# Which buffers the next weights take, when they are split, and how an opening is shared: a chain of residual blocks on one core

## The reference

```python
mod = (silu(c) @ w_mod + b_mod).reshape(-1, 9, 1024)          # and modc, the same from c_ctx
ada_in(x, mod, j, g)  = rmsnorm(x, g) * (1 + mod[3j+1]) + mod[3j]
ada_out(x, z, mod, j, g, r) = x + r * mod[3j+2] * rmsnorm(z, g)
x  = ada_out(x,  swiglu(ada_in(x,  mod,  0, ...), ffn_w_in, ffn_w_out), mod,  0, ..., 0.5)
xc = ada_out(xc, swiglu(ada_in(xc, modc, 0, ...), ffn_w_in, ffn_w_out), modc, 0, ..., 0.5)
...   # an mLSTM and pooling mixer over both, its output product w_out, a second swiglu
```

```python
x = x + 0.5 * rms_norm(swiglu_ffn(rms_norm(x, g0), w_gate, w_up, w_down), p0)
m = hybrid_mixer(rms_norm(x, g1), ...)     # ends in:
#   branch_d = einsum('bsgw,gwd->bsgd', branches, w_branch)     three branches
#   merged   = sum(sigmoid(gates) * branch_d, axis=2)
#   m        = merged @ w_out
x = x + rms_norm(m, p1)
x = x + 0.5 * rms_norm(swiglu_ffn(rms_norm(x, g2), ...), p2)
```

## Time and profile before

| | |
|---|---|
| median of three runs | 2121.56 us |
| the profiled execution | 2123.9 us |
| its span, first to last instruction | 2122.1 us |
| mean granted TensorE clock | 0.990 |
| TensorE busy | 2050.0 us (97%) |
| VectorE busy | 1320.1 us (62%) |
| ScalarE busy | 1034.8 us (49%) |
| DMA | 392.90 MB, 185 GB/s on average |

### The profile page before, as it was taken

How to read it: one execution, slowest core, us unless ns; L and a number is a source line. 1 busy time by engine, 2 the same in 40 slices (tenths; PEclk the granted TensorE clock), 3 DMA queues, 4 the chain that set the end, 5 groups by cost and what they waited for, 6 DMA issues and landing times. The chain is left out here.

```text
span 2122.1 us, 27560 instructions
## 1 busy us (share of the span) xinstructions
PE 2050.0 (97%) x11092; PEld 1720.9 (81%) x11092; DVE 1320.1 (62%) x2135; ACT 1034.8 (49%) x1444; POOL 25.9 (1%) x51
## 2 busy tenths in 40 slices
PE   7999999998989999999999989999999999998998
PEld 5899899987767787888897868888888898777886
DVE  3555656655774657555687786555655677877553
ACT  4445465435454544444535644444544535655442
POOL 1000000000000000000000000000000000000000
PEclk9999999999999999999999999999999999999999
DMA  9885576654256756655543465554756443365551
GB/s 353 274 286 180 198 237 209 203 196 161 80 179 209 242 174 194 203 170 187 193 150 105 138 208 178 181 179 149 239 179 217 165 140 124 120 218 165 190 183 49
DMA packets 281758, 392.90 MB, mean 185 GB/s; under 512 B 9580, under 2 KB 175900, under 8 KB 281504
## 3 DMA queue, kind: packets, MB, share of 16 engines
q1 hardware_dynamic: 277472, 379.62, 53.5%
q0 software_dynamic: 3184, 9.04, 1.4%
q10 hardware_dynamic: 976, 2.49, 0.3%
HBM read 390.06 MB, written 1.05 MB: 184 GB/s over the span
## 5 line engine op out<-in xcount | busy, mean ns | idle before, releaser
L1932 DVE TENSOR_TENSOR wlo<-raw,whi 128x1024 fp32r<-128x1024 f32 x650 | 781.3, 1222 | 491.1 <-ACT whi L1360 489.2
L1360 ACT ACTIVATE whi<-raw 128x1024 fp32r<-128x1024 f32 x650 | 673.0, 1056 | 605.7 <-PE bank L802 359.5
L800 PE MATMUL bank<-whi,xTh 128*128 128x512 f32 (+1 forms) x1344 | 535.2, 398 | 20.0 <-issue 6.8
L802 PE MATMUL bank<-whi,xTl 128*128 128x512 f32 (+1 forms) x1344 | 524.8, 390 | 0.0
L801 PE MATMUL bank<-wlo,xTh 128*128 128x512 f32 (+1 forms) x1344 | 524.8, 390 | 0.0
L800 PEld LDWEIGHTS bank<-whi,xTh 128*128 128x128 f32 x1344 | 255.8, 190 | 79.0 <-issue 15.5
L802 PEld LDWEIGHTS bank<-whi,xTl 128*128 128x128 f32 x1344 | 255.2, 190 | 53.8
L801 PEld LDWEIGHTS bank<-wlo,xTh 128*128 128x128 f32 x1344 | 255.8, 190 | 49.5
L764 PE MATMUL bank<-xTh,whi 128*128 128x256 f32 x696 | 198.1, 285 | 0.8 <-DVE wlo L1932 0.7
L764 PE MATMUL bank<-xTl,whi 128*128 128x256 f32 x696 | 196.9, 283 | 0.0
L764 PE MATMUL bank<-xTh,wlo 128*128 128x256 f32 x696 | 196.9, 283 | 0.0
(11 more groups left out here) (358 smaller groups left out, 2339.3 us busy)
## 6 DMA issues: line engine op xcount, KB each, us to landing
raw<-in_w_in SPq DMA_DIRECT2D x68, 1024.0 KB, 5.2
raw<-in_ffn_w_in SPq DMA_DIRECT2D x132, 512.0 KB, 6.7
raw<-in_ffn_w_gate SPq DMA_DIRECT2D x88, 512.0 KB, 4.2
raw<-in_ffn_w_up SPq DMA_DIRECT2D x88, 512.0 KB, 5.4
raw<-in_ffn_w_down SPq DMA_DIRECT2D x40, 1024.0 KB, 4.9
raw<-in_w_mod SPq DMA_DIRECT2D x36, 1024.0 KB, 6.9
raw<-in_ffn_w_out SPq DMA_DIRECT2D x30, 1024.0 KB, 5.1
raw<-in_w_out SPq DMA_DIRECT2D x12, 1024.0 KB, 4.9
```

Source lines behind the costliest of these rows:

```text
L800: e.matmul(o, hi[:, kc, sl], wh[:, c], start=at == 0 and k == 0, stop=False)
L802: ins = e.matmul(o, lo[:, kc, sl], wh[:, c], start=False, stop=fin)
L1360: e.activation(m.wh[t.slot[q]][:, 0:width], m.raw[:, u % NRAW, j * width:(j + 1) * width], ACT.Copy).then_inc(m.whi_done, 1)
L1932: e.tensor_tensor(m.wl[t.slot[q]][:, 0:width], m.raw[:, u % NRAW, j * width:(j + 1) * width], m.wh[t.slot[q]][:, 0:width].bitcast(F32), AL ...
```

## The change

Four edits. (1) `widen` gets an argument `due` apart from `at`, and slots 18 to 22 are added with the key q0 - 0.5 and the same due time, q0 + 2. (2) Both engines set `limit` to piece 5 before `last` of the output product, and `merge` lifts it when it ends. (3) In the opening, VectorE scales and shifts token tile 3 (and ScalarE only copies it), VectorE adds the first bias between its two normalizations, `mod` settles the one before it between its two halves, and TensorE settles behind each tile's transposes. (4) The modulation pieces ahead of groups 2 and 3 go ahead of groups 8 and 9; `x` is loaded behind group 3 and normalized beside groups 6 and 7; POOL loads the gains at k = 7.

```diff
-    def widen(self, slots, kind, key, at=None, once=False):
+    def widen(self, slots, kind, key, at=None, once=False, due=None):
         at = len(self.subs) if at is None else at
+        due = at if due is None else due
...
-                self.guard[s] = (b, n + 1, at, at - 0.5)
+                self.guard[s] = (b, n + 1, due, at - 0.5)
...   # Tables.walk (and TensorE's and VectorE's loops alike)
         for g in range(2, NG):
-            if 2 + g < EARLY:
-                self.mod(MODS[2 + g])
+            if 4 <= g < EARLY:
+                self.mod(MODS[g])
...   # Tables.mixer
-        self.widen((18, 19, 20, 21, 22), "bank", ("mg", l, 1, 1), q0 + 2, True)
+        self.widen((18, 19, 20, 21, 22), "bank", ("mg", l, 1, 1), q0, True, q0 + 2)
...   # Pool
-            if k == 6:
+            if k == 7:
...   # Tensor.mod
             ins.then_inc(full if kh else m.mod_half, 1)
-        self.settle()
+            if kh == 0:
+                self.settle()
...   # Tensor.first_block
                 self.turned(("sh0", 2 + i), half, m.zc[:, i, :])
-            self.settle()
+                self.settle()
...   # Scalar.first_block
-            for i in range(2):
-                self.shift(("sh0", 2 + i), half, 0, 1, m.cTh, i)
-        e.dma_start(m.x[:, :, :], ...).then_inc(m.ld_x, 16)
+            self.shift(("sh0", 2), half, 0, 1, m.cTh, 0)
+            full = m.fullb[:, self.n.half % 2, :].rearrange("p (c n) -> p c n", c=4)
+            self.evacuated("sh0", 3, half)
+            self.hi(m.cTh[:, 4 * half:4 * half + 4, 128:256], full)
+            self.n.half += 1
...
-            if g < 4:
-                self.normalize(m.x[:, g - 2, :], m.z[:, g - 2, :], loaded=m.ld_x)
+            if g == 3:
+                e.dma_start(m.x[:, :, :], ...).then_inc(m.ld_x, 16)
+            if g in (6, 7):
+                self.normalize(m.x[:, g - 6, :], m.z[:, g - 6, :], loaded=m.ld_x)
...   # Scalar.mixer and Vector.mixer
             # at the end of merge(half)
+            self.limit = len(self.t.subs)
...
+        self.limit = self.t.first["wo2", l, 0] + 5
         self.last(4, ...)
...   # Vector.first_block
-        for i in range(2):
-            self.normalize()
+        self.normalize()
+        self.mod()
+        self.normalize()
         for half in range(2):
+            if half:
+                self.mod()
             self.mod()
-            self.mod()
-            if half:
-                self.force(4)
-            self.settle()
-            self.force(2)
+            self.force(2 + 2 * half)
+            self.settle()
+            self.evacuated("mod2", half, 0)
+            self.evacuated("mod2", 2 + half, 0)
+            bank, free = self.filled("sh0", 3, half)
+            full = m.fullb[:, (self.n.half + 1) % 2, :].rearrange("p (c n) -> p c n", c=4)
+            if half:
+                e.wait_ge(m.xt_done, 2)
+            for c in range(4):
+                k = 4 * half + c
+                ins = e.tensor_scalar(full[:, c, :], bank[:, c * 128:c * 128 + 128], m.gcol[:, 0, 1, k:k + 1],
+                                      m.modc[:, 0, 0, 1, k:k + 1], ALU.mult, ALU.add)
+            ins.then_inc(free, 1)
```

More of the change, by code:

```diff
@@ L129, in widen @@
                 b, n = self.bank[key]
-                self.guard[s] = (b, n + 1, at, at - 0.5)
+                self.guard[s] = (b, n + 1, due, at - 0.5)
             else:
-                self.guard[s] = (kind, key, key + 2 if kind == "spent" else at, key + 0.5 if kind == "spent" else at - 0.5)
+                self.guard[s] = (kind, key, key + 2 if kind == "spent" else due, key + 0.5 if kind == "spent" else at - 0.5)
             if once:
@@ L1588, in first_block @@
             self.modulated(2 + half)
-            for i in range(2):
-                self.shift(("sh0", 2 + i), half, 0, 1, m.cTh, i)
-        e.dma_start(m.x[:, :, :], m.I["x"].rearrange("(t p) d -> p t d", p=128)).then_inc(m.ld_x, 16)
+            self.shift(("sh0", 2), half, 0, 1, m.cTh, 0)
[3 more added lines that the diff above has]
+            self.n.half += 1
         self.stream(8, between={5: lambda: self.hide("c", 0)})
@@ L1596, in first_block @@
             self.hide("c", g)
-            if g < 4:
-                self.normalize(m.x[:, g - 2, :], m.z[:, g - 2, :], loaded=m.ld_x)
+            if g == 3:
+                e.dma_start(m.x[:, :, :], m.I["x"].rearrange("(t p) d -> p t d", p=128)).then_inc(m.ld_x, 16)
+            if g in (6, 7):
+                self.normalize(m.x[:, g - 6, :], m.z[:, g - 6, :], loaded=m.ld_x)
         self.hidden("c", NG - 1)
@@ L2226, in first_block @@
         e.wait_ge(m.ld_cols, 16)
-        for i in range(2):
-            self.normalize()
+        self.normalize()
+        self.mod()
+        self.normalize()
         for half in range(2):
+            if half:
+                self.mod()
             self.mod()
-            self.mod()
-            if half:
-                self.force(4)
-            self.settle()
-            self.force(2)
+            self.force(2 + 2 * half)
[4 more added lines that the diff above has]
+            full = m.fullb[:, (self.n.half + 1) % 2, :].rearrange("p (c n) -> p c n", c=4)
+            if half:
+                e.wait_ge(m.xt_done, 2)
+            for c in range(4):
+                k = 4 * half + c
+                ins = e.tensor_scalar(full[:, c, :], bank[:, c * 128:c * 128 + 128], m.gcol[:, 0, 1, k:k + 1], m.modc[:, 0, 0, 1, k:k + 1],
+                                      ALU.mult, ALU.add)
+            ins.then_inc(free, 1)
             for i in range(2):
```

## The result

The changed kernel takes 2114.65 us (median of five runs, 2112.62 to 2116.05); the kernel before took 2124.21 on the same chip (2121.32 to 2125.24, five runs). The ratio is 0.9958, 95% interval 0.9944 to 0.9973: 8.9 us faster, the interval going from 5.7 to 11.9. The forecast was 10.9 us faster, 2110.7 against the 2121.56 of before. That 2121.56 was the median of three runs, and with five it is 2124.21, so the forecast lies nearer in its gain than in its time.

What follows compares the result with a forecast made beforehand. TensorE, busy 97% of the span, was taken to bound the kernel, so only ending its few waits or half clock helps. Terms -7.2 - 5.5 - 2.2 + 3.0 + 0.4 + 0.6 = -10.9 us gave 2110.7, range 2103 to 2116.

Steps and rivals of the forecast that it cites:

- the output product: Last product of the second block's mixers: 7.2 us gained in layer 0 and 5.5 in layer 1, sum 12.7.
- the opening: Opening chain on two engines: piece 4 at 45.1 us against 47.33, 2.2 us gained, bounds 1.0 and 3.0.
- the put-off loads: Modulation, x and gains deferred in the opening: 3.0 us lost, plus 0.4 and 0.6 in smaller terms.
- The buffers: Output product: single-use slots first, so VectorE's ten splits run without a gap, ending at 1263.6 instead of 1271.0.
- The split: Output product: splits stop after piece 4 until the merge is done; TensorE's 2.60 us wait before piece 4 goes.
- may leave less of it (up to 2 us each) or the same; I count nothing: TensorE's half clock after the transposes of x, both layers: a wait of 4 instead of 7 us may shorten it.
- TensorE's order binds, 29.0: Opening's first product: input complete at 28.4, but TensorE's own earlier work sets the start at 29.0, against 30.45.
- The crowd: Before group 5: late x, gains and w_k delay its weights to 97.4; TensorE loses 3 us, bounds 0 and 5.
- The smaller terms: Opening: +0.4 us for x's normalizations in groups 6, 7; +0.6 for half clock behind the 3 us wait.
- the deferred transfers did cost: Answers the rival that the opening's deferred transfers cost nothing: -14.5 us, 2107; chance 0.25.
- the raw data landed in 5.3 to 6.3 us and not in 8: Answers the rival of late data for pieces 12 to 14, both layers: 4.6 less, -6.3 us, 2115; chance 0.12.
- the buffers did come sooner: Answers the rival that single-use slots open too late, leaving -4.9 us, 2116.7; chance 0.06.

Runs made afterwards that it cites:

- the early weighing without the split: Changed kernel with x and gains loaded early, forced splits cut from 7, 7, 7 to 4, 6, 7, and the two limit lines removed: 2101.33 us, ratio 0.9894.
- the best version: Changed kernel with x and gains loaded early and forced splits cut from 7, 7, 7 to 4, 6, 7, limit lines kept: 2099.60 us, ratio 0.9878.

## Why the prediction was right, and where its working was not

The time, the sign and most steps came out. By the parts: the output product -10.6 by the runs (forecast -12.7), the opening -1.3 (-2.2), the put-off loads +2.3 (+4.0). They sum to -9.6, and the whole measured -8.9. So the forecast was 2.1 us too high in the first part, 0.9 in the second and 1.7 too severe in the third, and the errors partly cancel.

**The buffers.** Right. VectorE's ten splits end at 1265.03; the forecast of 1263.6, moved by the 0.8 us by which this run came later to the place (1248.44 for 1247.61), says 1264.4. The loads of `in_ffn_w_up` issued there (512 KB each) took 5.3, 5.5 and 6.3 us to land, near the 6.4 that was chosen over 8.0, and the two gaps of 0.29 and 0.62 us stand where 0.6 us of late data were forecast. The choice was right for this profile, not for every one: with `x` and the gains early, 7.0 and 7.7 us were measured. Against the same wait for `z`, `x` comes 6.9 us sooner in layer 0, forecast 7.4 and taken as 7.2, and 5.3 us in layer 1, forecast 5.5. Wait on `x`: about 4 forecast, 4.7 and 4.4 measured. The stretches shortened by 6.4 and 5.9 us (7.2 and 5.5).

**The split.** The arithmetic was right and the credit was wrong. The 2.60 us do go, and piece 5 is not late. The prediction saw that what is taken away before piece 4 comes back as wait on `x` ("a wait of about 4 us stays"), and so did not count it twice. But it did not draw the conclusion: with the buffers in place, the split has no gain of its own on this path, only the question of what it does to the clock. That was the line "may leave less of it (up to 2 us each) or the same; I count nothing". For the change as it is, nothing was nearly right: 6.8 us at half clock behind `x` in layer 0 as before, 3.4 less in layer 1. Against the kernel without the split, though, 2.6 and 1.3 us were lost there that need not be. A working by "who sets the end of this wait" would have asked it.

**The opening.** Near in every time: the first product at 28.80 us (29.0 forecast), the second half's splits at 35.59 (35.9), piece 4 at 44.44 (45.1). But "TensorE's order binds, 29.0" does not hold in the changed kernel's profile:

```profile
28.80 0.38 PE L766 MATMUL bank<-cTh,whi 128*128 128x256 f32 x1 [0.85 <-DVE cTl L1999]
```

There the clock was full from 22.6 us on, TensorE was through with the work ahead of it sooner and waited for its input, which came 0.3 us after the 28.4 of the forecast. In the profile of the edit alone the clock rose at 28.3 us and TensorE's order did bind, at 29.02 us without a wait. That both give about 29.0 is partly luck. The term of 2.2 us is 2.0 in the profile of the edit alone; in the runs 1.3, with an interval from 3.2 gained to 0.4 lost. VectorE's four operations on 128x128, unknown before and bounded by 0 and 1.5 us, are 1.37:

```profile
25.26 1.37 DVE L2253 TENSOR_SCALAR full<-bank,gcol,modc 128x128 f32<-128x128 f32 x4
```

I took 1.0. It did not matter, as ScalarE's four beside them took 1.51 us.

**The crowd.** Right in mechanism, 0.8 us large in size. ScalarE got the weights at 96.14 us (forecast 97.4), TensorE waited 2.22 us (3 forecast; 2.2 and 2.8 in the other two profiles with the same opening). The queues in 82 to 92 us of the changed kernel (packets, MB, share; q0 is POOL's, q1 SP's, q10 ScalarE's):

```profile
DMA packets 1797, 3.75 MB, mean 375 GB/s; under 512 B 151, under 2 KB 441, under 8 KB 1797
...
q1 hardware_dynamic: 1346, 2.39, 65.1%
q0 software_dynamic: 425, 1.31, 36.7%
```

POOL's three transfers, 1.31 MB, were issued at 82.7 to 84.3 us and landed by 92.8. SP's first two loads of `in_ffn_w_in` (512 KB each), issued ahead of them at 81.5 and 82.0, landed at 94.4 and 96.1. They do overtake, as the earlier trace rows had it. How they do shows best where both queues have work, here in 87 to 91 us:

```profile
q0 software_dynamic: 311, 1.03, 70.8%
q1 hardware_dynamic: 307, 0.43, 32.0%
```

The packets are nearly equal in number, as the 359 and 368 of the earlier trace rows were, but POOL's are larger (3.3 KB against 1.4 KB in the mean here), so that its queue moves 2.4 times the bytes of SP's. Without them and `x` the same weights were there 4.4 us sooner (91.71 for 96.14). The smaller terms, 0.4 for the normalizations and 0.6 for half clock behind the wait, were not measured one by one; behind the wait of 2.2 us at 98 us the clock's record shows no half clock, so the 0.6 was not spent here. Behind the 2.8 us of the kernel without the split it shows 3.4 us from 99.9, so this was a matter of the single execution. Of the rivals none held: the deferred transfers did cost; the raw data landed in 5.3 to 6.3 us and not in 8, which cost VectorE 0.9 us and not 2.2; and the buffers did come sooner.

One reading was incomplete. The two waits of 7.0 us on `x` were called TensorE's longest, but the kernel before also has one of 7.0 us on the first `w_mod` in the opening. No edit touches it, and nothing in the sum hangs on it.

## What to carry to other kernels

Before an edit that takes away a wait is credited, ask which engine sets the end of the next wait on the same chain: if that engine gains nothing, the idle time only moves, and here it moved into one wait behind which TensorE lost its full clock. Time two edits on one chain each alone as well as together; here 6.6 and 15.3 us made 10.6. And put a load where its queue is quiet: a transfer that nobody waits for delays those that somebody does.

## What the runs showed of the hardware

- In the output products, waits of 1.5 to 2.6 us mostly left TensorE at 2.4 GHz, but not always. The wait of 2.6 us before piece 4 stood twelve times in six profiles. Three of them had 3.4 us at half clock behind them, all in layer 0: in the kernel before, with the put-off loads alone, and in the early weighing without the split. Nine had none, the one in layer 1 before among them. Waits of 4.4 to 5.4 us had 3.4 or 6.8 us, one of 6.2 us and all of 7.0 us had 6.8 us. So the length of a wait alone does not say what the clock does.
- In the opening the clock rose to full at 22.6 us in the changed kernel's profile (eight matmuls of a modulation took 1.93 us at 19.41 and 1.06 us at 24.73), at 31.0 us in the one before, and at 28 to 31 us in all others but one; in that one, the best version, it rose at 22.0, fell at 28.8 and rose again at 32.2. The first 30 us are no place to compare two single profiles.
- Where POOL's and SP's queues both had work, they moved packets in equal number and not bytes: 359 and 368 packets with 1.19 and 0.72 MB in 42 to 47 us before, 311 and 307 with 1.03 and 0.43 MB in 87 to 91 us after. Of two loads in the same crowd, the one in the queue with the larger packets got the larger share.
